# SP issues the vectors' transfers, ScalarE's operands run one chunk ahead of its squares, and the first unit's remainder and the vectors' transposes stand later

## The chip, the core and the metric

The kernel runs on one core of a Trainium2 chip. The core has TensorE (PE), VectorE (DVE), ScalarE (ACT), GpSimd (POOL) and SyncE (SP), which run their own instruction streams and meet at semaphores. The metric is the device time of one execution in microseconds; the figure is the median of the runs.

## What is computed

A float32 layer of 512 tokens by 1024 features (sparse attention beside a gated convolution, cross attention and a gated feed-forward), followed by a second block of two layers (a state space mixer, a forgetting attention, two feed-forwards). The change touches the first norm and the first projection:

```python
def rmsnorm(x, g):
    xf = x.astype(jnp.float32)
    y = xf * lax.rsqrt(jnp.mean(xf * xf, axis=-1, keepdims=True) + EPS)
    return (y * g.astype(jnp.float32)).astype(x.dtype)

h = rmsnorm(x, norm_mix_g)
proj = h @ w_in
q, k, v, qi, ki, wi, glu = jnp.split(proj, cuts, axis=-1)
q = partial_rope(q.reshape(bsz, seq, A_HEADS, HEAD_DIM), cos, sin)
```

## The kernel before

Every engine's order is written out by hand, and every dependence is a semaphore. The activations lie with features on partitions: X has eight chunks (`KC`) of 128 features by 512 tokens. A projection is a row of units. A unit makes 128 output features: SP loads its weights into RAW (two slots), ScalarE rounds them into WH (`round_weights`, semaphore `w_hi`), GpSimd makes the rest WL = RAW - WH (`remainder`, `w_lo`), and TensorE sums WH by the rounded operand PH and WH by its rest PL over the eight chunks, sixteen matmuls, then WL by PH, eight more (`unit`). These are called the high matmuls and the remainder phase below. Up to unit 7 a unit is one column block of `w_in`. SP may load the weights of unit u only when WL of unit u - 2 is made.

In the head of the program the vectors (gains, biases, convolution taps: fifteen small inputs in `VECTORS`) are loaded as rows into VROW, and turned by TensorE into columns. `norm_mix_g` comes first, alone (`gain_in`), so that `vec_c` 1 lets the operands start; the others are turned by three transposes, VectorE copies them to VEC, and that is `vec_c` 2. x comes in four transfers into XROW. TensorE turns each chunk (`turn_x`), VectorE copies it to X (`x_ready`), ScalarE makes PH = X * gain rounded (`op_hi`) and the square SQ of the chunk, VectorE makes PL (`low`, `op_lo`), and GpSimd adds the square to SSQ (`add_square`, `sq_used`). SQ has two slots, so the square of chunk c waits for the sum of chunk c - 2. In `prepare` this wait stands ahead of PH too.

The norm's scale does not enter the operands. It is applied when a unit's result leaves PSUM: `column_sums` sums SSQ over partitions on TensorE, VectorE and ScalarE make the inverse root and a diagonal DIAG, `spread_scales` spreads it over partitions inside unit 1, between the high matmuls and the remainder phase, and VectorE copies it to RS. Then VectorE takes units 0 and 1 out of PSUM and goes on to the angles of the rotation (`angles`).

Behind the squares ScalarE rounds two constants, waits for `vec_c` 2, issues four small transfers that swap halves of the taps and biases (WSW, BSW), and then rounds the weights of unit 1.

Of the kernel before, what the change touches and what calls it, by code (L numbers as in the profile page):

```python
# [20 lines left out]
ACT = mybir.ActivationFunctionType  # L21
AX = mybir.AxisListType.X

P = 128
T = 512
TB = T // P
D = 1024
KC = D // P
# [49 lines left out]
ROWS = [0, 0, 0]  # L78
COLUMN = {}
# [47 lines left out]
def build_program(nc, A, out):  # L127
    ctx = ExitStack()
    with ctx:
# [12 lines left out]
        X = at("X", [P, KC, T], F32, 0)  # L142
        PH = at("PH", [P, KC, T], F32R, 16384)
        PL = at("PL", [P, KC, T], F32R, 32768)
# [48 lines left out]
        VROW = at("VROW", [P, 3, P], F32, 155648)  # L193
        POSI = at("POSI", [P, T], I32, 163840)
# [114 lines left out]
        IDENT, ROTM, TRI, ONES = (CST[:, i * P:(i + 1) * P] for i in range(4))  # L309
# [5 lines left out]
        def column(name, i):  # L315
            name, first = name if isinstance(name, tuple) else (name, 0)
            t, base = COLUMN[name][0], COLUMN[name][1] + first
            return VEC[:, t, bass.ds(base + i, 1)]
# [166 lines left out]
        def _(sp):  # L485
# [9 lines left out]
            for j, c in enumerate(IN_COLS):  # L495
                load(START["in"] + j, j % 2, w_in[:, :, c:c + P])
                if j == 1:
                    sp.dma_start(MROW[:], A["mem"][0].rearrange("(b p) d -> p b d", p=P)).then_inc(mem_in, 16)
            with sp.Fori(0, 4) as i:
                for s in range(2):  # L500
# [122 lines left out]
        def _(act):  # L623
# [6 lines left out]
            def prepare(norm, c, gain, hi, s, ready):  # L630

                square_free(norm, c)
                act.wait_ge(*ready)
                act.activation(hi, X[:, bass.ds(c, 1), :], ACT.Copy, scale=column(gain, c)).then_inc(op_hi, 1)
                act.activation(SQ[:, s, :], X[:, bass.ds(c, 1), :], ACT.Square).then_inc(sq_ready, 1)  # L635
# [10 lines left out]
                act.wait_ge(st_var, NORM[norm] + 1)  # L646
                act.activation(SDN, VN, ACT.Sqrt).then_inc(st_std, 1)

            for name, rows, t in VECTORS:
                r = COLUMN[name][1]  # L650
                flat = A[name] if len(A[name].shape) == 1 else A[name].rearrange(
                    "a b -> (a b)") if len(A[name].shape) == 2 else A[name].rearrange("a b c -> (a b c)")
                act.dma_start(VROW[r:r + rows, t, :], flat.rearrange("(r p) -> r p", p=P))\
                   .then_inc(gain_in if name == "norm_mix_g" else vec_in, 16)
            act.dma_start(POSI[:], A["positions"].to_broadcast([P, T])).then_inc(pos_in, 16)
            act.wait_ge(vec_c, 1)
            for c in range(KC):
                prepare("mix", c, "norm_mix_g", PH[:, c, :], c % 2, (x_ready, c + 1))
                if c == 3:
                    round_weights(0, 0)  # L660
            act.wait_ge(cst_in, 16)
# [586 lines left out]
        def _(pool):  # L1248
            def remainder(u, s, kc=KC):
                pool.wait_ge(w_hi, u + 1)  # L1250
                pool.tensor_tensor(WL[:, s, 0:kc], RAW[:, s, 0:kc], WH[:, s, 0:kc], ALU.subtract).then_inc(w_lo, 1)  # L1251
# [5 lines left out]
            def add_square(norm, c, s):  # L1257
                pool.wait_ge(sq_ready, SQUARES[norm] + c + 1)
                if isinstance(c, int) and c == 0:
                    if NORM[norm]:  # L1260
                        pool.wait_ge(st_sum, NORM[norm])
                    pool.tensor_copy(SSQ[:], SQ[:, s, :]).then_inc(sq_used, 1)
                else:
                    pool.tensor_tensor(SSQ[:], SSQ[:], SQ[:, s, :], ALU.add).then_inc(sq_used, 1)  # L1264
                pool.drain()  # L1265
# [4 lines left out]
            pool.memset(VSH[0][:].bitcast(F32), 0.0).then_inc(pad_zero, 1)  # L1270
            pool.memset(VSL[0][:].bitcast(F32), 0.0).then_inc(pad_zero, 1)
            for c in range(KC):
                add_square("mix", c, c % 2)
                if c == 3:
                    remainder(0, 0)
            for u in range(1, 4):
                remainder(u, u % 2)
            pool.wait_ge(wc_hi, 1)
# [330 lines left out]
        def _(pe):  # L1609
# [25 lines left out]
            def column_sums(norm):  # L1635

                pe.wait_ge(sq_used, SQUARES[norm] + dict(NORMS)[norm])
                if NORM[norm]:
                    pe.wait_ge(st_rs, NORM[norm])
                for b in range(TB):  # L1640
                    mm = pe.matmul(ST[:, b:b + 1], SSQ[:, b * P:(b + 1) * P], ONES[:, 0:1], start=True, stop=True)
                mm.then_inc(st_sum, 1)

            def spread_scales(norm):

                pe.wait_ge(st_diag, NORM[norm] + 1)
                pe.matmul(ST[:], ONES, DIAG[:], start=True, stop=True).then_inc(st_bc, 1)
# [12 lines left out]
            pe.transpose(ST[:, 0:KC], VROW[0:KC, 0, :], IDENT[0:KC, 0:KC]).then_inc(vec_t, 1)  # L1660
            for c in range(KC):
                turn_x(c)
            pe.wait_ge(vec_in, 16 * (len(VECTORS) - 1))
            pe.wait_ge(vec_c, 1)
            for t in range(3):
                mm = pe.transpose(ST[:, t * P:t * P + ROWS[t]], VROW[0:ROWS[t], t, :], IDENT[0:ROWS[t], 0:ROWS[t]])
            mm.then_inc(vec_t, 1)

            def rotate(j):
                rows = P if j not in (0, 3) else 64  # L1670
# [37 lines left out]
                    mm.then_inc(mem_t, 1)  # L1708

            unit(0, 0, PH, PL, chunks=(op_lo, NOPERAND["mix"]))  # L1710
            pe.wait_ge(vec_c, 2)
            column_sums("mix")
            unit(1, 1, PH, PL, between=lambda: spread_scales("mix"))
            unit(2, 0, PH, PL)
            turn_weights_in()
            rotate(0)
# [1432 lines left out]
```

## Time and profile before

| | us |
|---|---|
| median of 3 runs | 2082.72 |
| lowest and highest | 2082.22, 2085.34 |
| profiled execution, whole | 2086.91 |
| its span, first to last instruction | 2085.1 |

The rows of the trace are times in microseconds from the start of the span: when a group of instructions starts, how long it takes, its engine, its line in the kernel, the operation, and in brackets how long the engine had been idle before it and what ended that. An engine name with a q (ACTq, SPq) is the queue that issues a transfer. TensorE's durations are modelled and overlap; the distance between two starts is the time that one takes of the engine. Matmuls are named by the buffers: PH,WH and PL,WH are the high matmuls, PH,WL the remainder phase.

### The profile page before, as it was taken

To read this page: it belongs to the slowest core of one execution; us is meant where nothing else is said; L and a number is where in the kernel's file an instruction comes from. 1 tells how busy PE (TensorE), PEld (TensorE's weight loads), DVE (VectorE), ACT (ScalarE), POOL (GpSimd) and SP (SyncE) were. 2 spreads that over 40 slices of the span, in tenths; PEclk is the share of its full clock that TensorE was granted. 3 is DMA by queue.
4 is the path that set the end of the run, shared out by engine and by line. 5 is a ranking of instruction groups with operands and counts; after the bars stand their busy time and mean duration, and the time that the engine had idled before them with its cause. 6 is when DMAs were issued, how large, how long until landed. Compare 5 with 4: busy or idle time off the path is not lost.

```text
span 2085.1 us, 31481 instructions
## 1 busy us (share of the span) xinstructions
PE 1975.9 (95%) x10763; PEld 1628.5 (78%) x10763; DVE 1053.7 (51%) x1640; ACT 742.7 (36%) x1263; POOL 1058.9 (51%) x591
## 2 busy tenths in 40 slices
PE   8989888999999999789999999999999899999997
PEld 5678866778877888567778888887878788888886
DVE  6797743745687686798342213132126723122132
ACT  4335444443322223445432222233237732222223
POOL 5575626536756644690554444446445264444442
PEclk9999999999999999999999999999999999999999
DMA  4334103142333332100323333334346333333332
GB/s 136 80 109 110 26 25 89 54 81 85 97 101 90 96 96 80 51 2 13 101 81 101 93 99 95 96 93 107 92 116 144 91 99 94 91 100 93 99 96 85
DMA packets 345028, 181.87 MB, mean 87 GB/s; under 512 B 28527, under 2 KB 336103, under 8 KB 344935
## 3 DMA queue, kind: packets, MB, share of 16 engines
q1 hardware_dynamic: 343872, 179.91, 31.4%
q8 instruction: 55, 0.90, 0.2%
q10 hardware_dynamic: 1062, 0.75, 0.1%
q14 instruction: 39, 0.31, 0.0%
HBM read 162.73 MB, written 2.10 MB: 79 GB/s over the span
## 4 chain that ended last, share of the span: by engine, by line
PE 56%; issue 12%; DVE 9%; POOL 8%; POOLq 5%; ACT 3%; DVEq 3%; DMA 1%; SPq 1%; ACTq 0%
PE ACC L1621 16%; PE ACC L1627 15%; PE ACC L1622 15%; POOL WL L1251 7%; POOLq L1265 2%; DVE SC L2410 1%; POOLq L1475 1%; POOLq L1463 1%; PE ACC L1793 1%; PE ST L2093 1%; DVE M L2407 1%; POOL GC L1474 1%; PE O L1750 1%; PE ST L1750 1%; PE O L1752 1%
## 5 line engine op out<-in xcount | busy, mean ns | idle before, releaser
L1251 POOL TENSOR_TENSOR WL<-RAW,WH 128x1024 fp32r<-128x1024 f32 (+1 forms) x292 | 691.6, 2371 | 738.3 <-ACT WH L628 680.8
L1621 PE MATMUL ACC<-PH,WH 128*128 128x512 f32 x1248 | 494.4, 396 | 7.0 <-DVE PL L2203 1.6
L1622 PE MATMUL ACC<-PL,WH 128*128 128x512 f32 x1248 | 488.6, 391 | 0.0
L628 ACT ACTIVATE WH<-RAW 128x1024 fp32r<-128x1024 f32 (+1 forms) x292 | 300.8, 1032 | 452.9 <-PE ACC L1627 402.4
L1621 PE MATMUL ACC<-QH,WH 128*128 128x512 f32 (+1 forms) x1136 | 430.2, 383 | 19.9 <-ACT WH L628 10.4
L1622 PE MATMUL ACC<-QL,WH 128*128 128x512 f32 (+1 forms) x1136 | 425.4, 379 | 0.0
L1627 PE MATMUL ACC<-PH,WL 128*128 128x512 f32 x1248 | 312.7, 393 | 0.0
L1621 PEld LDWEIGHTS ACC<-PH,WH 128*128 128x128 f32 x1248 | 235.8, 189 | 65.1 <-issue 4.8
L1627 PE MATMUL ACC<-QH,WL 128*128 128x512 f32 (+1 forms) x1136 | 271.7, 380 | 9.6 <-POOL WL L1251 6.4
L1627 PEld LDWEIGHTS ACC<-PH,WL 128*128 128x128 f32 x1248 | 235.1, 189 | 52.8 <-issue 3.3
L1622 PEld LDWEIGHTS ACC<-PL,WH 128*128 128x128 f32 x1248 | 235.8, 189 | 48.7 <-issue 1.0
L1621 PEld LDWEIGHTS ACC<-QH,WH 128*128 128x128 f32 x1136 | 214.7, 189 | 70.0 <-issue 14.5
L1627 PEld LDWEIGHTS ACC<-QH,WL 128*128 128x128 f32 x1136 | 205.7, 189 | 53.9 <-POOL WL L1251 10.9
L1622 PEld LDWEIGHTS ACC<-QL,WH 128*128 128x128 f32 x1136 | 214.9, 189 | 38.4 <-issue 0.2
L3020 DVE TENSOR_TENSOR X<-X,ACC 128x512 f32 x48 | 33.0, 687 | 216.3 <-PE ACC L1627 216.3
L3010 DVE TENSOR_TENSOR H<-ACC,RS 128x512 f32<-128x512 f32 x64 | 44.3, 692 | 149.1 <-PE ACC L1627 148.6
L1264 POOL TENSOR_TENSOR SSQ<-SSQ,SQ 128x512 f32<-128x512 f32 x51 | 74.3, 1458 | 69.2 <-ACT SQ L635 64.3
L876 ACT ACTIVATE QH<-H 128x512 f32 (+1 forms) x54 | 34.1, 632 | 158.2 <-DVE H L3012 128.3
L2496 DVE TENSOR_TENSOR PTL<-ACC,PTH 128x128 fp32r<-128x128 f32 (+2 forms) x112 | 53.4, 476 | 37.3 <-ACT PTH L816 36.9
L816 ACT ACTIVATE PTH<-ACC 128x128 fp32r<-128x128 f32 (+2 forms) x112 | 47.8, 427 | 60.6 <-PE O L1752 36.8
L876 ACT ACTIVATE PH<-H 128x512 f32 (+1 forms) x32 | 20.2, 632 | 128.3 <-DVE H L3012 128.3
L2832 DVE TENSOR_TENSOR QL<-H,QH 128x512 f32 x54 | 37.4, 693 | 49.4 <-ACT QH L876 49.4
(450 smaller groups left out, 2566.4 us busy)
## 6 DMA issues: line engine op xcount, KB each, us to landing
RAW<-in_mlp_w_dram SPq DMA_DIRECT2D x128, 512.0 KB, 4.0
RAW<-in_w_gate_dram SPq DMA_DIRECT2D x22, 512.0 KB, 3.7
RAW<-in_w_up_dram SPq DMA_DIRECT2D x22, 512.0 KB, 3.8
RAW<-in_w_in_dram SPq DMA_DIRECT2D x16, 512.0 KB, 3.9
RAW<-in_w_down_dram SPq DMA_DIRECT2D x16, 512.0 KB, 4.0
RAW<-in_ssm_w_glu_dram SPq DMA_DIRECT2D x16, 512.0 KB, 3.8
RAW<-in_w_kvf_dram SPq DMA_DIRECT2D x16, 512.0 KB, 3.9
RAW<-in_w_out_dram SPq DMA_DIRECT2D x16, 256.0 KB, 2.8
```

The source lines that it names most:

```text
L628: act.activation(WH[:, s, 0:kc], RAW[:, s, 0:kc], ACT.Copy).then_inc(w_hi, 1)
L816: act.activation(parts(kind, t // TB)[0][:, first:first + kb, qb * P:(qb + 1) * P], TT[t % 2][:, 0:kb * P].rearrange("p (k q) -> p k q", q ...
L876: act.activation(hi[:, bass.ds(k, 1), :], to, ACT.Copy).then_inc(hid_hi, 1)
L1251: pool.tensor_tensor(WL[:, s, 0:kc], RAW[:, s, 0:kc], WH[:, s, 0:kc], ALU.subtract).then_inc(w_lo, 1)
L1264: pool.tensor_tensor(SSQ[:], SSQ[:], SQ[:, s, :], ALU.add).then_inc(sq_used, 1)
L1265: pool.drain()
L1621: pe.matmul(ACC[s][:, 0:n], WH[:, s, k, :], xh[:, k, :], start=(k == 0), stop=False)
L1622: pe.matmul(ACC[s][:, 0:n], WH[:, s, k, :], xl[:, k, :], start=False, stop=False)
L1627: mm = pe.matmul(ACC[s][:, 0:n], WL[:, s, k, :], xh[:, k, :], start=False, stop=(k == kc - 1))
L1750: pe.matmul(out, ah, bh, start=first, stop=False)
L2496: dve.tensor_tensor(pair[1][to], TT[t % 2][:, 0:kb * P].rearrange("p (k q) -> p k q", q=P), pair[0][to], ALU.subtract).then_inc(pt_lo, 1)
L3010: dve.tensor_tensor(h[:], ACC[s][:], RS[:], ALU.mult).then_inc(unit_out, 1)
```

## The change

Four things move; no arithmetic is added or removed.

- The transfers of fourteen vectors and of the positions go from ScalarE's queue to SP's, behind the weights of units 0 and 1 and ahead of `mem`. `norm_mix_g` stays on ScalarE's queue.
- ScalarE makes PH of chunk c + 1 ahead of the square of chunk c, and only the square waits for its slot.
- GpSimd makes the remainder of unit 0 after six sums of squares instead of four.
- TensorE turns the vectors behind unit 0 instead of ahead of it, and the column sums go from between units 0 and 1 into unit 1, ahead of its fifth chunk.

```diff
@@ SP
                 if j == 1:
+                    for name, rows, t in VECTORS:
+                        r = COLUMN[name][1]
...
+                        if name != "norm_mix_g":
+                            sp.dma_start(VROW[r:r + rows, t, :], flat.rearrange("(r p) -> r p", p=P)).then_inc(vec_in, 16)
+                    sp.dma_start(POSI[:], A["positions"].to_broadcast([P, T])).then_inc(pos_in, 16)
                     sp.dma_start(MROW[:], A["mem"][0].rearrange("(b p) d -> p b d", p=P)).then_inc(mem_in, 16)
@@ ScalarE
-            for name, rows, t in VECTORS:
...
-            act.dma_start(POSI[:], A["positions"].to_broadcast([P, T])).then_inc(pos_in, 16)
+            act.dma_start(VROW[0:KC, 0, :], A["norm_mix_g"].rearrange("a b -> (a b)").rearrange("(r p) -> r p", p=P)).then_inc(gain_in, 16)
             act.wait_ge(vec_c, 1)
-            for c in range(KC):
-                prepare("mix", c, "norm_mix_g", PH[:, c, :], c % 2, (x_ready, c + 1))
+            for c in range(KC + 1):
+                if c < KC:
+                    act.wait_ge(x_ready, c + 1)
+                    act.activation(PH[:, c, :], X[:, c, :], ACT.Copy, scale=column("norm_mix_g", c)).then_inc(op_hi, 1)
+                if c:
+                    square("mix", c - 1, X, (c - 1) % 2)
                 if c == 3:
                     round_weights(0, 0)
@@ GpSimd
             for c in range(KC):
+                if c == 6:
+                    remainder(0, 0)
                 add_square("mix", c, c % 2)
-                if c == 3:
-                    remainder(0, 0)
@@ TensorE
-            pe.wait_ge(vec_in, 16 * (len(VECTORS) - 1))
-            pe.wait_ge(vec_c, 1)
-            for t in range(3):
-                mm = pe.transpose(ST[:, t * P:t * P + ROWS[t]], VROW[0:ROWS[t], t, :], IDENT[0:ROWS[t], 0:ROWS[t]])
-            mm.then_inc(vec_t, 1)
+            def turn_vectors():
...
+            def first_sums():
+                pe.wait_ge(vec_c, 2)
+                column_sums("mix")
             unit(0, 0, PH, PL, chunks=(op_lo, NOPERAND["mix"]))
-            pe.wait_ge(vec_c, 2)
-            column_sums("mix")
-            unit(1, 1, PH, PL, between=lambda: spread_scales("mix"))
+            turn_vectors()
+            unit(1, 1, PH, PL, inside=(4, first_sums), between=lambda: spread_scales("mix"))
```

On TensorE, at the end of unit 0 and the start of unit 1 (ST<-CST,SSQ are the column sums), before:

```order
L1627 MATMUL ACC<-PH,WL 128x512 x8
L1641 MATMUL ST<-CST,SSQ 128x1 x4
L1621 MATMUL ACC<-PH,WH 128x512
L1622 MATMUL ACC<-PL,WH 128x512
L1621 MATMUL ACC<-PH,WH 128x512
```

And now, from the remainder phase of unit 0 to the fifth chunk of unit 1 (ST<-CST,VROW are the vectors' transposes):

```order
L1632 MATMUL ACC<-PH,WL 128x512 [waits w_lo]
L1632 MATMUL ACC<-PH,WL 128x512 x7
L1672 MATMUL ST<-CST,VROW 128x100 [waits vec_c,vec_in]
L1672 MATMUL ST<-CST,VROW 128x124
L1672 MATMUL ST<-CST,VROW 128x88
L1626 MATMUL ACC<-PH,WH 128x512 [waits w_hi]
...
L1627 MATMUL ACC<-PL,WH 128x512
L1646 MATMUL ST<-CST,SSQ 128x1 [waits sq_used,vec_c]
L1646 MATMUL ST<-CST,SSQ 128x1 x3
```

The transposes stand between the two units now, and four chunks of unit 1 stand ahead of the sums.

On ScalarE, the middle of the chunks, before:

```order
L634 ACTIVATE PH<-X,VEC 128x512 [waits x_ready,sq_used]
L635 ACTIVATE SQ<-X 128x512
L628 ACTIVATE WH<-RAW 128x1024 [waits w_landed0]
L634 ACTIVATE PH<-X,VEC 128x512 [waits x_ready,sq_used]
L635 ACTIVATE SQ<-X 128x512
```

And now, from there to the weights of unit 1:

```order
L661 ACTIVATE PH<-X,VEC 128x512 [waits x_ready]
L650 ACTIVATE SQ<-X 128x512 [waits sq_used]
L635 ACTIVATE WH<-RAW 128x1024 [waits w_landed0]
...
L650 ACTIVATE SQ<-X 128x512 [waits sq_used] x2
L667 ACTIVATE PAIR<-CST 128x128 [waits cst_in]
L668 ACTIVATE PAIR<-CST 128x128
L672 DMA WSW<-VEC 64x124 [waits vec_c]
L673 DMA BSW<-VEC 64x4
L672 DMA WSW<-VEC 64x124
L673 DMA BSW<-VEC 64x4
L635 ACTIVATE WH<-RAW 128x1024 [waits w_landed1]
```

The wait for the slot went from PH to SQ. The rows from PAIR to WH are the same as before; the `vec_c` that they wait for comes from the transposes above.

## Rows read from the trace of the kernel before

**Rows 1.** The page: the chain that ended last, by engine.

```profile
PE 56%; issue 12%; DVE 9%; POOL 8%; POOLq 5%; ACT 3%; DVEq 3%; DMA 1%; SPq 1%; ACTq 0%
```

**Rows 2.** The chain in order of time, 25 to 60: start, us, what.

```profile
25.67 3.33 PE ACC L1627 x8
...
34.43 1.87 PE ACC L1627 x8
...
37.99 0.43 DVE COS L2287
...
38.50 2.67 DVE COS L2289
...
58.22 0.70 PE FOUR L1696 x4
```

**Rows 3.** Timeline of TensorE, 13 to 37.

```profile
17.08 0.73 PE L1666 MATMUL ST<-CST,VROW 100*128 100x100 f32 x3
17.53 0.78 PE L1621 MATMUL ACC<-PH,WH 128*128 128x512 f32 x1
...
21.94 0.40 PE L1621 MATMUL ACC<-PH,WH 128*128 128x512 f32 x1
...
24.86 0.50 PE L1621 MATMUL ACC<-PH,WH 128*128 128x512 f32 x1 [0.97 <-DVE PL L2203]
...
28.84 0.95 PE L1641 MATMUL ST<-CST,SSQ 128*128 128x1 f32 x8
29.65 0.47 PE L1621 MATMUL ACC<-PH,WH 128*128 128x512 f32 x1
```

**Rows 4.** Busy time by window; behind POOL's stands the granted clock (PEclk).

```profile
26.00:27.00 1.00, 1.00 (x4) 0.81 (x3) 0.00 (x0) 0.00 (x0) 0.00 (x0) 0.50 0.13 32
```

**Rows 5.** Timeline of ScalarE and its queue, 7 to 30.

```profile
7.58 0.43 ACTq L655 DMA_DIRECT2D POSI<-in_positions_dram  x1
8.09 1.28 ACT L634 ACT_TABLE_LOAD   x1 [8.09 <-DVE X L2249]
...
14.58 1.06 ACT L628 ACTIVATE WH<-RAW 128x1024 fp32r<-128x1024 f32 x1
...
16.15 0.61 ACT L635 ACTIVATE SQ<-X 128x512 f32<-128x512 f32 x1
...
21.15 0.72 ACT L634 ACTIVATE PH<-X,VEC 128x512 fp32r<-128x512 f32 x1 [3.23 <-POOL SSQ L1264]
...
25.35 0.53 ACTq L667 DMA_DIRECT2D WSW<-VEC  x1
...
27.86 1.06 ACT L628 ACTIVATE WH<-RAW 128x1024 fp32r<-128x1024 f32 x1 [3.62 <-issue]
```

**Rows 6.** Timeline of VectorE, 6 to 37.

```profile
6.57 0.69 DVE L2249 COPY X<-FOUR 128x512 f32<-128x512 f32 x1 [2.39 <-PE FOUR L1655]
...
15.44 0.68 DVE L2249 COPY X<-FOUR 128x512 f32<-128x512 f32 x1
...
24.73 0.59 DVE L2256 COPY VEC<-ST 128x92 f32<-128x92 f32 x3
...
31.42 0.69 DVE L2235 TENSOR_TENSOR DIAG<-CST,ST 128x512 f32<-128x512 f32 x1
```

**Rows 7.** Timeline of GpSimd, 6 to 39.

```profile
15.12 1.52 POOL L1264 TENSOR_TENSOR SSQ<-SSQ,SQ 128x512 f32<-128x512 f32 x1 [0.16 <-issue]
16.81 2.62 POOL L1251 TENSOR_TENSOR WL<-RAW,WH 128x1024 fp32r<-128x1024 f32 x1 [0.16 <-issue]
...
38.49 2.40 POOL L1251 TENSOR_TENSOR WL<-RAW,WH 128x1024 fp32r<-128x1024 f32 x1 [4.66 <-ACT WH L628]
```

**Rows 8.** Timeline of SP's queue, 0 to 40.

```profile
3.34 4.30 SPq L489 DMA_DIRECT2D RAW<-in_w_in_dram  x2
```

**Rows 9.** DMA of 0 to 30: GB/s in 40 slices, and RAW: KB, median us to landing.

```profile
GB/s 0 0 100 272 308 336 241 317 341 359 376 378 333 306 290 295 305 314 338 375 386 311 158 66 16 0 0 80 255 322 42 0 0 0 0 42 1 43 1 0
...
RAW<-in_w_in_dram SPq DMA_DIRECT2D x3, 512.0 KB, 11.2
```

More of the change, by code:

```diff
@@ L497, in _ @@
                 if j == 1:
+                    for name, rows, t in VECTORS:
+                        r = COLUMN[name][1]
+                        flat = A[name] if len(A[name].shape) == 1 else A[name].rearrange(
+                            "a b -> (a b)") if len(A[name].shape) == 2 else A[name].rearrange("a b c -> (a b c)")
+                        if name != "norm_mix_g":
+                            sp.dma_start(VROW[r:r + rows, t, :], flat.rearrange("(r p) -> r p", p=P)).then_inc(vec_in, 16)
+                    sp.dma_start(POSI[:], A["positions"].to_broadcast([P, T])).then_inc(pos_in, 16)
                     sp.dma_start(MROW[:], A["mem"][0].rearrange("(b p) d -> p b d", p=P)).then_inc(mem_in, 16)
@@ L647, in standard_deviation @@
                 act.activation(SDN, VN, ACT.Sqrt).then_inc(st_std, 1)
-            for name, rows, t in VECTORS:
[L650 to L654, printed above, removed]
-            act.dma_start(POSI[:], A["positions"].to_broadcast([P, T])).then_inc(pos_in, 16)
-            act.wait_ge(vec_c, 1)
-            for c in range(KC):
-                prepare("mix", c, "norm_mix_g", PH[:, c, :], c % 2, (x_ready, c + 1))
+            act.dma_start(VROW[0:KC, 0, :], A["norm_mix_g"].rearrange("a b -> (a b)").rearrange("(r p) -> r p", p=P)).then_inc(gain_in, 16)
+            act.wait_ge(vec_c, 1)
+            for c in range(KC + 1):
[4 more added lines that the diff above has]
+                    square("mix", c - 1, X, (c - 1) % 2)
                 if c == 3:
@@ L1662, in _ @@
                 turn_x(c)
-            pe.wait_ge(vec_in, 16 * (len(VECTORS) - 1))
-            pe.wait_ge(vec_c, 1)
-            for t in range(3):
-                mm = pe.transpose(ST[:, t * P:t * P + ROWS[t]], VROW[0:ROWS[t], t, :], IDENT[0:ROWS[t], 0:ROWS[t]])
-            mm.then_inc(vec_t, 1)
+            def turn_vectors():
+                pe.wait_ge(vec_in, 16 * (len(VECTORS) - 1))
+                pe.wait_ge(vec_c, 1)
+                for t in range(3):
+                    mm = pe.transpose(ST[:, t * P:t * P + ROWS[t]], VROW[0:ROWS[t], t, :], IDENT[0:ROWS[t], 0:ROWS[t]])
+                mm.then_inc(vec_t, 1)
+            def first_sums():
+                pe.wait_ge(vec_c, 2)
+                column_sums("mix")
             def rotate(j):
```

## The prediction

> **What bounds the kernel now.** The page comes first: the chain that ended last lies to 56% on TensorE [rows 1]. The change touches only the head of the program, so the head's part of that chain is read next [rows 2]. It passes through the remainder phase of unit 0 (25.67), through unit 1 up to the end of its remainder phase (34.43 + 1.87 = 36.30), then through VectorE, which takes unit 1 out and makes the angles (37.99, 38.50), and it is back on TensorE at 58.22. So one number decides: the time at which unit 1 ends, 36.30 now. What follows hangs on it by waits of one engine on another, with nothing tied to an absolute time; I pass a shift on one to one.
>
> How 36.30 comes about is read backwards in the timelines. Unit 1's first matmul is at 29.65, right behind the column sums of 28.84, which stand behind unit 0's remainder phase [rows 3]. That phase took 3.33 us where the same eight matmuls of unit 1 take 1.87 [rows 2], because the granted clock was 0.50, the 1.2 GHz level [rows 4]. TensorE had waited before it for VectorE's PL (the last wait 0.97 us, [rows 3]), because ScalarE's seventh PH had waited 3.23 us for GpSimd's SSQ [rows 5]: GpSimd was in the 2.62 us remainder of 16.81 [rows 7].
>
> **1. Vectors leave ScalarE's queue.** ScalarE issues DMAs until 8.01 and loads its table at 8.09 [rows 5]. X of chunk 0 is ready at 6.57 + 0.69 = 7.26 [rows 6]. With one DMA to issue it starts at 7.3: 0.8 us earlier, PH of chunk 0 at 8.6. The fourteen vectors and POSI now stand on SP's queue behind the second RAW load, whose issue ends at 3.34 + 4.30 = 7.64 [rows 8]. At 0.43 us each, as for POSI [rows 5], their issue lasts to 14.1 and the transfer of `mem`, behind them, is issued 6.4 us later. With the 11.2 us that the crowded loads took [rows 9] it lands at 25, against a use on ScalarE beyond 31, and the vectors are wanted at 25.4 (below). Both are hidden, at no cost.
>
> The 0.42 MB of vectors and POSI no longer run beside x and RAW of unit 0. RAW 0 was issued at 3.34 and landed 11.2 later, at 14.54 [rows 8, 9], and ScalarE's rounding of it begins at 14.58 [rows 5]: it waited for the transfer. At 300 GB/s, about the mean of the slices up to 14 us (241 to 378), 0.42 MB (304 rows of 512 bytes and 128 copies of 2 KB) are 1.4 us, so the landing lies between 13.2 and 14.5; I take the middle, 13.9. The Trainium skill, page "DMA: Bandwidth & Descriptors", section "Issuing engines are not separate DMA queues", says that DMAs of different issuers run on the same 16 engines and interleave, so that moving an issue saves only the sequencer's time. By it the landing is 13.2; were the queues apart, it stays 14.5, and every time of the next step moves by 0.7 with it.
>
> **2. PH ahead of the square, remainder later.** ScalarE reaches the rounding of unit 0 at 13.2 and stands there until 13.9. From the start of that rounding to the end of the next square it takes 16.15 + 0.61 - 14.58 = 2.18 us [rows 5], so the square of chunk 3 ends at 16.1. GpSimd then adds squares 3, 4 and 5 back to back, 1.69 us apart (15.12 to 16.81, [rows 7]), and the remainder starts at 21.2. With the 2.40 of a remainder in the clear (38.49) it ends at 23.6. TensorE: X of chunk 5 was copied at 15.44 [rows 6] and goes with the head by 0.8, so unit 0 starts at about 16.6 in place of 17.53. There are eleven matmuls between 17.53 and 21.94, 0.43 apart, and at the full clock they stand 1.87 / 8 = 0.23 apart. Of sixteen, ten at 0.43 and six at 0.23 or 0.43 end between 22.3 and 23.5. PL is ready: VectorE takes 1.7 us a chunk, so from X of chunk 5 at 14.6 the last PL is done near 21. The remainder phase therefore waits for GpSimd until 23.6 and takes 1.87 at the full clock: unit 0 ends at **25.4**, where it ended at 29.0. That is the gain, 3.6 us.
>
> **3. The vectors' transposes behind unit 0.** Here it is given back. ScalarE's order is not changed behind the squares: it waits for `vec_c` 2, issues four DMAs, and only then rounds the weights of unit 1. Before, VEC was copied at 24.73, the first of the DMAs began at 25.35 and the rounding at 27.86 [rows 5, 6], all beside unit 0's slow remainder phase. Now the transposes (0.73 us, 17.08 in [rows 3]) follow unit 0, the copies (0.59) follow them, then 27.86 - 25.35 = 2.51 of issues and 1.06 of rounding: 25.4 + 0.73 + 0.59 + 2.51 + 1.06 + 0.15 for four handovers = **30.4**. Unit 1 starts 0.75 us later than before. TensorE is idle from 26.1 to 30.4, and queued behind unit 1 on it is all the rest.
>
> **4. The sums inside unit 1.** Before, the chain from the sums (ended 28.84 + 0.95 = 29.79) to DIAG (31.42 + 0.69 = 32.11, [rows 6]) ran under unit 1's sixteen high matmuls, 3.8 us, free of charge. Now it has only the last eight, 1.86 us, as cover, and it takes 2.32. The spread takes 0.9, what is left of the 36.30 - 29.65 = 6.65 us of unit 1 without its 3.8 and 1.87. Unit 1: 1.86 + 0.7 for the sums (the 0.95 lies partly at the low clock) + 2.3 + 0.9 + 1.87 = 7.65 us in place of 6.65. That is +1.0. The sums' own 0.7 is no new work, it stood ahead of the unit before.
>
> **5. The clock.** TensorE's idle 4.3 us ahead of unit 1 have no like in the head. The nearest row is the drop to 0.50 after a stretch in which it was only partly idle [rows 3, 4], so I expect unit 1 to start at 1.2 GHz. Such a spell lasted 3.0 us (about 25.5 to 28.5) and, at the start, 4.4 us (17.53 to 21.94); half of it is lost, 1.5 to 2.2. Part of it falls into the wait for DIAG: I take **+1.7**; the ends are 0 and 2.5. The Trainium skill, "TensorE: Matmul & The Clock Gate", Part 1, says "the default state is throttled, and activity releases the throttle". By it the 1.7 stands; with the clock held it would be 0 and the sum 1.75.
>
> **Sum.** 0.75 + 1.0 + 1.7 = +3.45 us: unit 1 ends at 39.75 instead of 36.30. The profiled execution took 2086.9 around its span of 2085.1 and would become 2090.4; it lies 4.2 above the median of the runs, 2082.7, and the median would become **2086.2**.
>
> **Rivals.**
> *The clock holds.* The idle stretch is too short, or the engine recovers in the first matmuls. For it: the drop before came only after several gaps, of which the last was 0.97. Against it: 4.3 us in one piece. +1.75 us, 2084.5.
> *Slow through unit 1* (the other side). If the low level outlasts the first half, the sums and all twenty-four matmuls run at 0.43 instead of 0.23: 24 x 0.2 = 4.8 in place of 1.7, and the sum is 0.75 + 1.0 + 4.8 = +6.55, 2089.3. It decides from a spell of over 7 us on. GpSimd's remainder of unit 3 works the same way from another side: one VectorE step of the angles lies under it and takes 2.67 us where the like step ahead of it takes 0.43 (38.50, 37.99 in [rows 2]; the remainder is 38.49 in [rows 7]). Another alignment catches two such steps, +2.2, or none, -2.2.
> *The gain stays.* If the four DMA issues take the 0.43 us of POSI's each, 1.7 in place of 2.51, unit 1 starts at 29.6, and with the clock held and no collision with the angles the sum is 3.45 - 0.8 - 1.7 - 2.2 = -1.25, 2081.5. A gain beyond 4 us needs more still.
> *It doesn't do what it says.* If the vectors land after 25.4, behind two RAW loads, TensorE waits for them: 1 us of lateness costs 1 us. RAW 1 is issued by 7.64 and, 11.2 later, through by 18.8 at the latest, and they are small; some 6 us are in hand.
>
> **How the numbers follow.** Forecast 0.50 (+1.7 to +4.8), clock holds 0.20, slow through unit 1 or two collisions 0.20, gain stays 0.07, late vectors 0.03. A measurement of this kernel tells about 0.2%, 4.2 us, from no change. Of the forecast 0.08 lie beyond it; with 0.20 and 0.02 that is slower 0.30. Faster by 4.2 us has no mechanism here beyond the unknown alignments: 0.05. The rest, 0.65, is within. Low end: the gain-stays case, -1.25; high end: the slow spell, +6.55. With 0.4 of scatter below, 2081.0, and the rest of it left out above, 2089.2.
>
> **What would show it.** In the profile of the changed kernel: table load at about 7.3; rounding of unit 0 at 13.2 to 14.5; no wait of PH on SSQ; the remainder of unit 0 ending near 23.6; a TensorE gap of some 4 us ahead of unit 1, its matmuls 0.43 apart at first; a wait for DIAG in unit 1; its end near 39.75. Wrong would be: the rounding of unit 1 ahead of the transposes, or a shift at 36 us that is not found at 58 us and at the end.

## The result and the profile after

The kernel after takes 2092.07 us (median of 5 runs, 2091.69 to 2093.04), the kernel before 2082.72 in the same rounds (5 runs, 2081.86 to 2087.06): ratio 1.0040, with an interval of 1.0027 to 1.0052. It is slower by more than the 0.2% that the prediction counted as no change, and 5.9 us above the predicted 2086.2, beyond the range's 2089.2. Later rounds put it at 1.0027 (1.0017 to 1.0036). Between medians the loss is 9.4 us in the first rounds and 5.9 in the later ones; 5.9 above 2082.7 would lie just inside the range. The profiled execution took 2091.69 around a span of 2089.9.

The mechanism that the prediction named is there. The timeline of TensorE from unit 0 to unit 2, after (the lines left out are matmuls of the same units; compare [rows 3]):

```profile
17.14 0.78 PE L1626 MATMUL ACC<-PH,WH 128*128 128x512 f32 x1
...
24.43 0.50 PE L1626 MATMUL ACC<-PH,WH 128*128 128x512 f32 x1 [2.04 <-DVE PL L2212]
...
25.00 2.00 PE L1632 MATMUL ACC<-PH,WL 128*128 128x512 f32 x8
26.84 0.44 PE L1672 MATMUL ST<-CST,VROW 100*128 100x100 f32 x3
31.56 0.80 PE L1626 MATMUL ACC<-PH,WH 128*128 128x512 f32 x1 [4.29 <-ACT WH L635]
32.16 0.63 PE L1627 MATMUL ACC<-PL,WH 128*128 128x512 f32 x1
32.59 0.63 PE L1626 MATMUL ACC<-PH,WH 128*128 128x512 f32 x1
...
35.15 1.70 PE L1646 MATMUL ST<-CST,SSQ 128*128 128x1 f32 x8
...
40.27 1.43 PE L1652 MATMUL ST<-DIAG,CST 128*128 128x512 f32 x2
41.13 2.39 PE L1632 MATMUL ACC<-PH,WL 128*128 128x512 f32 x8
43.50 0.47 PE L1626 MATMUL ACC<-PH,WH 128*128 128x512 f32 x1
```

Unit 0 ends at 26.84 (before: 28.84, both read at the start of what follows its remainder phase). Then TensorE waits 4.29 us for the rounded weights of unit 1, and unit 1 runs from 31.56 to 43.50: 11.94 us, where it was 6.6 (29.65 in [rows 3] to 36.3). Its high matmuls stand 0.43 apart. The granted clock, by window (the columns are us, busy time of PE, PEld, DVE, ACT and POOL, then PEclk, DMA share and GB/s):

```profile
30.00:31.00 1.00, 0.00 (x0) 0.00 (x0) 0.00 (x0) 0.55 (x1) 0.00 (x0) 0.92 0.13 32
31.00:36.00 5.00, 4.44 (x13) 3.67 (x14) 0.00 (x0) 1.79 (x2) 2.37 (x1) 0.50 0.16 32
36.00:40.00 4.00, 4.00 (x12) 3.32 (x13) 1.55 (x6) 2.83 (x5) 1.71 (x1) 0.50 0.31 92
...
41.00:42.00 1.00, 1.00 (x4) 0.57 (x3) 0.27 (x1) 0.00 (x0) 0.00 (x0) 0.96 0.20 26
```

A window of 1 us with a mean between the two levels tells where the edge lies: 0.92 is a fall 0.16 us before its end, at 30.84, and 0.96 a rise 0.08 us behind its start, at 41.08. So the clock falls to 1.2 GHz in the idle stretch and is back at 2.4 GHz 10.2 us later, 9.5 us into the unit: it stays low through all sixteen high matmuls, the sums and the spread, although TensorE is busy from 31.56 on without a break.

Why unit 1 started at 31.56 stands on ScalarE and its queue, after (compare [rows 5]):

```profile
7.46 1.28 ACT L661 ACT_TABLE_LOAD   x1 [7.46 <-DVE X L2258]
...
13.61 1.04 ACT L635 ACTIVATE WH<-RAW 128x1024 fp32r<-128x1024 f32 x1
...
27.95 0.53 ACTq L672 DMA_DIRECT2D WSW<-VEC  x1
...
29.79 0.62 ACTq L673 DMA_DIRECT2D BSW<-VEC  x1
30.45 1.06 ACT L635 ACTIVATE WH<-RAW 128x1024 fp32r<-128x1024 f32 x1 [8.15 <-issue]
```

ScalarE's operands no longer wait for GpSimd (the 3.23 us of [rows 5] are gone), and the engine has nothing to do for 8.15 us but wait for `vec_c` 2 and issue four transfers, with the weights of unit 1 unrounded behind them. On VectorE, the last three PL, the vectors' copies and DIAG, after:

```profile
18.33 1.17 DVE L2212 SCALAR_TENSOR_TENSOR PL<-X,VEC,PH 128x512 fp32r<-128x512 f32 x1
...
20.03 4.35 DVE L2212 SCALAR_TENSOR_TENSOR PL<-X,VEC,PH 128x512 fp32r<-128x512 f32 x2
27.31 0.60 DVE L2265 COPY VEC<-ST 128x92 f32<-128x92 f32 x3 [2.94 <-PE ST L1672]
...
38.28 0.69 DVE L2244 TENSOR_TENSOR DIAG<-CST,ST 128x512 f32<-128x512 f32 x1
```

The view of the tile PL, of 21.3 to 21.6, splits the pair of 20.03 (minimum, median and maximum in ns, first and last start): the last PL began at 21.5 and took 2.85 us, until 20.03 + 4.35 = 24.38.

```profile
L2212 DVE SCALAR_TENSOR_TENSOR PL<-X,VEC,PH x2: 1577/2212/2848, 20.0 to 21.5; 128x512 fp32r<-128x512 f32 x2
```

And on GpSimd, the remainder of unit 0, after (compare [rows 7]):

```profile
21.21 2.61 POOL L1256 TENSOR_TENSOR WL<-RAW,WH 128x1024 fp32r<-128x1024 f32 x1 [0.16 <-issue]
```

The shift at the end of unit 1, 43.5 - 36.3 = +7.2, is found again where [rows 2] ended. In the chain of waits, after, the line that stood at 58.22 is 7.0 us later:

```profile
65.24 0.70 PE FOUR L1706 x4
```

The first transposes of `mem` also come 7.0 us later (97.16 before, 104.16 after). Beyond them the two executions do not keep this distance: at the sums of the next norm it is 2.7 us, and at the end 4.8. Those sums, before and then after:

```profile
357.28 0.95 PE L1641 MATMUL ST<-CST,SSQ 128*128 128x1 f32 x8
```

```profile
359.94 0.95 PE L1646 MATMUL ST<-CST,SSQ 128*128 128x1 f32 x8
```

The change does not touch this stretch. From the first transposes of `mem` to these sums the profiled executions of all kernels here take between 254.3 and 260.1 us (before 260.1 and 259.4, after 255.8 and 256.2), so a difference of the order of the effect comes from there. The mean granted clock of 200 to 300 us was 0.90 in the execution of before and 0.93 in that of after. A single pair of spans therefore doesn't measure the change. The medians do (+9.4 and +5.9), and up to 97 us the heads do.

### The profile page after: what moved, and what is told of

It is laid out like the page before. It is cut to its first block, busy times and chain, and to the rows that moved or that the text cites. A ratio compares the mean times of both kernels' runs of the same rounds, so it can differ in the third digit from the quotient of the medians.

```text
span 2089.9 us, 31475 instructions
## 1 busy us (share of the span) xinstructions
PE 1977.1 (95%) x10763; PEld 1628.8 (78%) x10763; DVE 1051.8 (50%) x1640; ACT 743.0 (36%) x1263; POOL 1058.8 (51%) x591
## 4 chain that ended last, share of the span: by engine, by line
PE 55%; issue 13%; POOL 10%; DVE 7%; POOLq 6%; ACT 3%; DVEq 2%; DMA 2%; SPq 1%; ACTq 0%
PE ACC L1626 16%; PE ACC L1627 15%; PE ACC L1632 15%; POOL WL L1256 7%; POOLq L1270 2%; POOLq L1480 1%; POOLq L1468 1%; PE ACC L1802 1%; PE ST L2102 1%; POOL GC L1479 1%; PE ST L1759 1%; PE O L1759 1%; ACT WH L635 1%; PE O L1761 1%; POOL GT L1467 1%
## 5 line engine op out<-in xcount | busy, mean ns | idle before, releaser
L1626 PE MATMUL ACC<-PH,WH 128*128 128x512 f32 x1248 | 497.1, 398 | 11.5 <-ACT WH L635 4.5
L881 ACT ACTIVATE PH<-H 128x512 f32 (+1 forms) x32 | 20.2, 632 | 128.3 <-DVE H L3021 128.3
```

What stands on the lines that cost most here:

```text
L881: act.activation(hi[:, bass.ds(k, 1), :], to, ACT.Copy).then_inc(hid_hi, 1)
L1626: pe.matmul(ACC[s][:, 0:n], WH[:, s, k, :], xh[:, k, :], start=(k == 0), stop=False)
```

## The experiments

Names: the "head" of a run is the start of unit 2's first matmul in its profile, when unit 1 is done (before 36.2, after 43.5). The theory: TensorE's late transposes make the whole loss, through the wait for `vec_c` 2 that holds up the rounding of unit 1, and the low clock behind that wait. Rivals: the loss comes from the other parts (SP's queue, ScalarE's or GpSimd's order), or from the sums inside unit 1. Each ratio is to the kernel before in the same rounds, where its median was 2083.87 to 2084.04.

**before_again**: the kernel before, unchanged, as a control.

> The kernel before, unchanged, for a second execution with a profile. The profile shown of before took 2086.9 us, 4.2 above the median of its runs. If the head alone makes the difference between the two kernels, unit 1 ends at 36.3 us here too, and what executions of before differ in lies further on, in the spells of the low clock between 180 and 295 us, of which a quick execution should show fewer. If instead the head of the shown execution was unusual, unit 1 ends elsewhere than at 36.3 by more than 1 us.

Measured: 2084.02 (2080.88 to 2086.80), ratio 1.0004 (0.9995 to 1.0013). Its executions scatter by 6 us. In this one unit 0's remainder phase ran at the full clock, and the head is at 34.95, not 36.2:

```profile
24.81 1.98 PE L1627 MATMUL ACC<-PH,WL 128*128 128x512 f32 x8
26.63 0.95 PE L1641 MATMUL ST<-CST,SSQ 128*128 128x1 f32 x8
28.36 0.50 PE L1621 MATMUL ACC<-PH,WH 128*128 128x512 f32 x1 [0.78 <-ACT WH L628]
```

So the slow remainder phase of [rows 2], from which the prediction read the gain of step 2, is met in some executions only. In the shown execution of before its row is:

```profile
25.47 3.54 PE L1627 MATMUL ACC<-PH,WL 128*128 128x512 f32 x8
```

It was worth less than it seemed: here unit 1 waits for ScalarE even with the fast phase.

**round1_first**: the weights of unit 1 rounded ahead of the wait for `vec_c` 2.

```diff
+            round_weights(1, 1)
             act.wait_ge(vec_c, 2)
...
-            rounded(1)
```

> The changed kernel with one line moved: ScalarE rounds the weights of unit 1 behind the two constants and ahead of the wait for the vectors' columns and the four small transfers. Theory that these issues, behind the late transposes, hold unit 1: the rounding runs at about 22.3 to 23.4, unit 1 starts right behind the transposes at 27.6, in place of 31.56, the clock stays up, unit 1 takes 7.7 us in place of 11.9 and ends near 35.3 to 36, so the time falls by 7 to 8 us against the changed kernel, to about 2084, near before. Rival, that the two units are held apart by the transposes and sums on TensorE itself: less than 2 us gained.

Measured: 2085.30 (2078.79 to 2089.37), ratio 1.0005 (0.9995 to 1.0016); head 36.16. TensorE, with nothing idle ahead of unit 1 and now a wait inside it:

```profile
26.39 0.44 PE L1672 MATMUL ST<-CST,VROW 100*128 100x100 f32 x3
26.62 0.48 PE L1626 MATMUL ACC<-PH,WH 128*128 128x512 f32 x1
...
33.23 1.12 PE L1652 MATMUL ST<-DIAG,CST 128*128 128x512 f32 x2 [1.79 <-DVE DIAG L2244]
```

One line moved on ScalarE takes 7.3 us from the head and brings the time back to that of before. So most of what the late transposes cost in the head goes through the rounding behind the issues. Not all of it: the four issues (27.51 to about 29.97) stand now ahead of the square root of the norm, whose table load begins at 30.00, and DIAG is late for it. With TensorE's old order and the same rounding (early_round1 below) the head is 1.9 us earlier and the median 4.9 lower. Only the 1.9 is seen in the head; the profiled execution of round1_first took 2081.08, 4.2 below its median, and where the rest of the 4.9 lies isn't shown.

**gap_filled**: the kernel after with eighteen superfluous matmuls behind the transposes, in what was idle time. Their result is overwritten.

```diff
             turn_vectors()
+            for _ in range(18):
+                pe.matmul(ACC[1][:], WH[:, 0, 0, :], PH[:, 0, :], start=True, stop=True)
```

> The changed kernel with 18 extra matmuls (first weights of unit 0 by the first chunk, into the bank that unit 1 starts over) between the transposes and unit 1; the wait for the weights of unit 1 stays. 18 x 0.23 = 4.1 us fill the gap of 4.3 us, so that unit 1 still starts at 31.6 to 31.8. Theory that the low clock through unit 1 costs 4 us more than the wait itself: the clock stays at 2.4 GHz, unit 1 takes 7.7 us and ends at 39.3, the time falls by 4 us to about 2088. Rival, that the idle stretch alone is the price and the clock is only seen beside it: no gain, or a loss.

Measured: 2087.22 (2085.91 to 2089.44), ratio 1.0018 (1.0009 to 1.0027). The matmuls fill the wait and unit 1 follows at once, at the full clock:

```profile
28.09 4.55 PE L1723 MATMUL ACC<-PH,WH 128*128 128x512 f32 x18
32.67 0.50 PE L1626 MATMUL ACC<-PH,WH 128*128 128x512 f32 x1
...
40.69 0.47 PE L1626 MATMUL ACC<-PH,WH 128*128 128x512 f32 x1
```

```profile
32.00:36.00 4.00, 3.96 (x22) 3.08 (x21) 0.17 (x1) 2.08 (x4) 2.39 (x1) 1.00 0.03 4
```

Unit 1 takes 8.0 us instead of 11.9, so the clock costs it 3.9 us. Unit 1 starts 1.1 us later than in after, 0.8 of it because unit 0 ended later (27.65; its remainder phase was slow in this execution, 3.23 us), and the head is 2.8 earlier. With the wait filled, the clock holds through unit 1. In the three executions with 4.29 us of idle time ahead of unit 1 (after, after_again, turns_late_only) and in sums_outside, with 2.54, unit 1 began at the low clock; in the others, with 0.78 at most, at the full one. So unit 1's clock goes with the idle time ahead of it here, though a fall also came with less: at 25.1 in this run, at 25.4 in before, behind waits of 2.04 and 0.97 us, and in turns_late_only at 24.2, ahead of the 4.29. In medians the gain is smaller and less sure than in the head: 2.5 us against the later rounds of after, with intervals that overlap (1.0009 to 1.0027 and 1.0017 to 1.0036), and 4.9 against the first.

**turns_early**: the kernel after with TensorE's order as it was before (transposes ahead of unit 0, sums between the units).

```diff
+            pe.wait_ge(vec_in, 16 * (len(VECTORS) - 1))
+            pe.wait_ge(vec_c, 1)
...
             unit(0, 0, PH, PL, chunks=(op_lo, NOPERAND["mix"]))
-            turn_vectors()
-            unit(1, 1, PH, PL, inside=(4, first_sums), between=lambda: spread_scales("mix"))
+            first_sums()
+            unit(1, 1, PH, PL, between=lambda: spread_scales("mix"))
```

> The changed kernel with TensorE's order as before: the vectors' transposes ahead of unit 0, the column sums between units 0 and 1. The vectors still come over SP's queue. Theory that the late transposes hold the weights of unit 1: rounding of unit 1 ends before unit 0 does, and unit 1 starts right behind the sums at about 28 to 29; against that the transposes wait for vectors that SP issued last at 15.5, to land at 17.5 to 18.5, so unit 0 starts 1 us later. Unit 1 ends near 36, 7 us earlier than changed, time 2084 to 2086. Rival, that the gain is lost to SP's queue: the transposes wait until after 20 and unit 1 ends beyond 38.

Measured: 2080.58 (2078.80 to 2082.57), ratio 0.9988 (0.9979 to 0.9996): faster than before, 9.2 and 11.5 us below the two medians of after, and 3.4 below the low end of what was expected. Its head:

```profile
23.80 0.50 PE L1626 MATMUL ACC<-PH,WH 128*128 128x512 f32 x1 [1.61 <-DVE PL L2211]
...
24.37 2.00 PE L1632 MATMUL ACC<-PH,WL 128*128 128x512 f32 x8
27.91 0.50 PE L1626 MATMUL ACC<-PH,WH 128*128 128x512 f32 x1 [0.40 <-ACT WH L635]
...
34.49 0.47 PE L1626 MATMUL ACC<-PH,WH 128*128 128x512 f32 x1
```

The three other parts are a small gain, and TensorE's part undoes it. Unit 1 is again released by ScalarE's WH, as in before_again. The head explains only a part of the 3.4 us between the medians: it is 1.7 us earlier than in the shown execution of before and 0.5 earlier than in before_again.

**turns_late_only**: the kernel before with TensorE's part of the change alone.

```diff
             unit(0, 0, PH, PL, chunks=(op_lo, NOPERAND["mix"]))
-            pe.wait_ge(vec_c, 2)
-            column_sums("mix")
-            unit(1, 1, PH, PL, between=lambda: spread_scales("mix"))
+            turn_vectors()
+            unit(1, 1, PH, PL, inside=(4, first_sums), between=lambda: spread_scales("mix"))
```

> The kernel before with TensorE's part of the change alone: transposes behind unit 0, sums inside unit 1; vectors on ScalarE's queue, the squares and the remainder as before. Theory that TensorE's part makes the whole loss: the weights of unit 1 come behind unit 0, transposes, copies and four issues, unit 1 starts 4.7 us after unit 0 at 31.5 to 33.7, runs at the low clock and ends at 43.5 to 45.5; time 2092 to 2094, as changed or a little above. Rival, that the loss needs the vectors on SP's queue or the late remainder: below 2088.

Measured: 2091.77 (2090.05 to 2093.70, 6 runs), ratio 1.0036 (1.0023 to 1.0048), as slow as the whole change. The wait for WH is again 4.29 us, with everything but TensorE's order as in before:

```profile
34.43 0.80 PE L1621 MATMUL ACC<-PH,WH 128*128 128x512 f32 x1 [4.29 <-ACT WH L628]
...
37.96 0.95 PE L1641 MATMUL ST<-CST,SSQ 128*128 128x1 f32 x8
...
44.01 0.47 PE L1621 MATMUL ACC<-PH,WH 128*128 128x512 f32 x1
```

With turns_early this settles where the loss comes from, from both sides. The low clock ended here 3.4 us into unit 1, ahead of the sums (0.95 us for them, where after has 1.70), but it had been low since 24.2, through unit 0's remainder phase (3.62 us), 13.6 us in all.

**sums_outside**: the kernel after with the sums ahead of unit 1, in the idle time.

```diff
             turn_vectors()
-            unit(1, 1, PH, PL, inside=(4, first_sums), between=lambda: spread_scales("mix"))
+            first_sums()
+            unit(1, 1, PH, PL, between=lambda: spread_scales("mix"))
```

> The changed kernel with the column sums ahead of unit 1 (behind the transposes) instead of inside it; everything else, the gap ahead of unit 1 too, stays. In the changed kernel unit 1 starts at 31.6 and the clock is back up only at about 40.7; the sums stand in the middle, 1.6 us of one-column matmuls. Theory that the sums inside the unit prolong the slow spell: with sixteen matmuls in one piece the clock is up after 3 to 5 us, the second half runs at 0.23 apart, unit 1 ends at 39.5 to 40.5, 3 to 4 us earlier than changed, time near 2088.5. Rival, that the spell after such a gap lasts 9 us whatever follows: only the 1.6 us of the sums leave unit 1, it ends near 42, time near 2090.5.

Measured: 2088.35 (2082.91 to 2091.04), ratio 1.0019 (1.0009 to 1.0028); head 40.70.

```profile
31.40 0.79 PE L1626 MATMUL ACC<-PH,WH 128*128 128x512 f32 x1 [2.54 <-ACT WH L635]
...
40.70 0.47 PE L1626 MATMUL ACC<-PH,WH 128*128 128x512 f32 x1
```

Unit 1 starts when it did, still slow, but takes 9.3 us in place of 11.9. 1.6 of the 2.6 are the sums, which lie in idle time now; the rest is the clock, low from 30.4 to 37.3, 6.8 us instead of 10.2:

```profile
37.00:38.00 1.00, 1.00 (x5) 0.78 (x5) 0.00 (x0) 0.00 (x0) 0.00 (x0) 0.87 0.56 104
```

In these heads the place of the sums is a second, smaller part of the loss. The medians do not show it: 2088.35 lies 1.4 us below the later median of after, and the intervals overlap. The head was a little later than the 39.5 to 40.5 expected.

**after_again**: the kernel after, unchanged, as a control.

> The changed kernel once more, for a second execution with a profile and for its time beside before in the same rounds. In its first profile the slow spell of unit 1 lasted from before 31 to 40.7, across the sums; with the sums ahead of the unit it ended at 37.1, with them inside but a remainder phase that was slow already it ended at 37.6. If the long spell belongs to the sums' place, unit 1 ends at 43 to 44 again. If the end of a spell falls by chance, unit 1 ends anywhere between 39.5 and 44, and the times of the rounds scatter by 3 us or more. In the rounds of the first result they lay within 1.4 us of each other, which speaks for the former. Expected: 2091 to 2093.

Measured: 2089.76 (2086.32 to 2093.99, 12 runs), ratio 1.0027 (1.0017 to 1.0036). The head is at 42.57. Unit 1 starts at 31.12 and the clock is low from 29.4 to 39.6, again 10.2 us, but 1.7 of them lie in the idle stretch where the first execution had 0.7:

```profile
29.00:30.00 1.00, 0.00 (x0) 0.00 (x0) 0.00 (x0) 0.00 (x0) 0.00 (x0) 0.69 0.05 3
39.00:40.00 1.00, 1.00 (x4) 0.79 (x3) 0.00 (x0) 1.00 (x2) 1.00 (x1) 0.69 0.00 0
```

The spell has the same length in both executions of this code, and what differs is when it begins. The time is below the 2091 to 2093 expected, and the executions scatter by 8 us, where the expectation named a scatter of 3 us or more as the sign that a spell's end falls by chance; the head, 42.57, lies between its two cases. Two equal lengths don't rule the chance out.

**early_round1**: turns_early and round1_first together. Beside the edit of turns_early:

```diff
+            round_weights(1, 1)
             act.wait_ge(vec_c, 2)
...
-            rounded(1)
```

> The kernel with SP's vectors, ScalarE's order and the late remainder, TensorE's order as before, and the rounding of unit 1's weights ahead of the wait for the vectors' columns. Without it (turns_early) TensorE waited 0.4 us for that rounding at 27.9. Theory: unit 1 starts at 27.5, right behind the sums, the rest of it is bound by matmuls; 0.4 us gained, time about 2080.2. Rival, that ScalarE's four issues now stand between the rounding and the square root (the table load waits behind them) and DIAG comes late: no gain or 1 us lost.

Measured: 2080.39 (2079.13 to 2084.66), ratio 0.9984 (0.9975 to 0.9993); head 34.23, unit 1 starts at 27.68.

**early_remainder4**: turns_early with the remainder of unit 0 after four sums of squares, as before, to let VectorE's last PL go free.

```diff
-                if c == 6:
+                if c == 4:
                     remainder(0, 0)
```

> turns_early with the remainder of unit 0 after four sums of squares, as before, instead of six. In turns_early the last PL of VectorE stands behind that remainder and TensorE waits 1.6 us for it at 23.8. Theory that the late remainder only moves the collision of VectorE and GpSimd from one PL to another: the remainder at 17.2 holds up PL of chunk 5 and the X behind it instead, the last PL comes at the same time within 0.5 us, time 2080 to 2081.5. If the late remainder was a gain by itself, it is 1 us or more slower; if it was a loss, 1 us or more faster.

Measured: 2080.28 (2079.18 to 2084.45), ratio 0.9987 (0.9978 to 0.9996); head 34.61. TensorE's wait for the last PL falls from 1.61 to 0.95 us, but the PL that now lies under the remainder is an earlier one, and the remainder phase starts at 24.45, as in turns_early:

```profile
18.18 2.26 DVE L2211 SCALAR_TENSOR_TENSOR PL<-X,VEC,PH 128x512 fp32r<-128x512 f32 x1
```

**early_both**: turns_early with the edits of both.

```diff
+            round_weights(1, 1)
             act.wait_ge(vec_c, 2)
...
-            rounded(1)
@@ GpSimd
-                if c == 6:
+                if c == 4:
                     remainder(0, 0)
```

> early_round1 and early_remainder4 together: SP's vectors, ScalarE's order, remainder of unit 0 after four sums, rounding of unit 1 ahead of the wait for the vectors' columns, TensorE's order as before. If what each of the two brings is real and separate, the last PL comes at 23.9, unit 1 starts at 27.4 and ends near 34; time 2079.5 to 2080.5. If nothing is left to gain in this stretch, it equals turns_early within 0.5 us.

Measured: 2080.41 (2077.41 to 2084.27), ratio 0.9991 (0.9982 to 1.0001); head 33.92. The three versions and turns_early have heads 0.7 us apart at most and medians within 0.3 us; they can't be told apart by their times. The gain over before is in what they share.

**vectors_sp_only**: the kernel before with the vectors' and positions' transfers on SP, as in the change, and nothing else.

```diff
@@ SP
                 if j == 1:
+                    for name, rows, t in VECTORS:
...
+                    sp.dma_start(POSI[:], A["positions"].to_broadcast([P, T])).then_inc(pos_in, 16)
@@ ScalarE
-            for name, rows, t in VECTORS:
...
-            act.dma_start(POSI[:], A["positions"].to_broadcast([P, T])).then_inc(pos_in, 16)
```

> The kernel before with the vectors and positions issued by SP alone; ScalarE's order, the remainder and TensorE's order as before. Theory that turns_early's gain of 3.4 us comes from both parts: here ScalarE's table load starts at 7.4 in place of 8.1, the rounding of unit 0 at 13.5 in place of 14.6, but PH of chunk 6 still waits for GpSimd's sums behind the remainder. Unit 0 starts 0.3 to 0.7 us earlier, unit 1 ends at 34.5 to 36; time 2082 to 2084. Rival, that this part makes the whole gain: 2080 to 2081.

Measured: 2082.11 (2079.59 to 2085.35), ratio 0.9992 (0.9983 to 1.0001); head 35.56, both as expected. Its table load still begins at 8.09: here x came late (the copy of chunk 0 began at 7.31 and ended at 8.00, where it ended at 7.26 in before), and not the queue held ScalarE. PH waits for GpSimd as before:

```profile
21.16 0.72 ACT L641 ACTIVATE PH<-X,VEC 128x512 fp32r<-128x512 f32 x1 [3.24 <-POOL SSQ L1265]
```

**order_only**: the kernel before with ScalarE's and GpSimd's orders of the change.

```diff
@@ ScalarE
-            for c in range(KC):
-                prepare("mix", c, "norm_mix_g", PH[:, c, :], c % 2, (x_ready, c + 1))
+            for c in range(KC + 1):
...
+                if c:
+                    square("mix", c - 1, X, (c - 1) % 2)
@@ GpSimd
+                if c == 6:
+                    remainder(0, 0)
                 add_square("mix", c, c % 2)
-                if c == 3:
-                    remainder(0, 0)
```

> The kernel before with ScalarE's order (PH ahead of the last chunk's square) and the late remainder alone; vectors on ScalarE's queue, TensorE's order as before. Theory as above: ScalarE starts at 8.1, PH no longer waits for sums, the last PL still collides with the remainder. Unit 1 ends at 34.5 to 36; time 2081 to 2083. Rival, that the order makes the whole gain of turns_early: 2080 to 2081.

Measured: 2082.64 (2078.52 to 2086.51), ratio 0.9995 (0.9984 to 1.0007); head 34.79, both as expected. The collision that was expected did not come: in this run the last PL was nearly done when the late remainder began (21.88), and TensorE waited for the remainder itself:

```profile
24.54 2.11 PE L1631 MATMUL ACC<-PH,WL 128*128 128x512 f32 x8 [1.48 <-POOL WL L1255]
```

The two parts alone are 1.8 and 1.2 us below before's median of 2083.9 and neither is clear of no change; together (turns_early) they make 3.4 (2083.95 to 2080.58). Beside before_again's head of 34.95 those of the two, 35.56 and 34.79, show no gain.

## Why the prediction was wrong

The sum was 0.75 + 1.0 + 1.7 = +3.45 at the end of unit 1. The measured shift is +7.2. It passed on one to one, as assumed, at 58 and at 97 us. At the end of the two shown executions it is +4.8, so the shift at 36 us is not found whole at the end, which the prediction had named as a sign of being wrong. What stands behind that is the scatter between 97 us and the end, which the sum did not have. By its steps:

**Step 1 was right in its results, and one reading in it was wrong.** The table load began at 7.46 (7.3 said), the rounding of unit 0 at 13.61 (13.9 said), and vectors and `mem` were hidden: no unit waited for a vector, though SP's issues of vectors and positions lasted to 15.85 and not to 14.1. But the rounding of before did not wait for the transfer, as the step said. Its row has no idle time, and it begins where the square ahead of it ends (13.95 + 0.61 = 14.56):

```profile
13.95 0.61 ACT L635 ACTIVATE SQ<-X 128x512 f32<-128x512 f32 x1
```

In after too it stands right behind a square, with no idle time. That 13.61 is near 13.9 is luck. In before_again the rounding did wait for RAW (0.74 us, until 14.71).

**Step 2 was right about GpSimd and wrong about VectorE.** The remainder ran from 21.21 to 23.82, against 21.2 to 23.6. But the step said "the last PL is done near 21": it was done at 24.38. A part of this is that X did not come earlier: chunk 5 was copied at 15.64 (14.6 said, 15.44 before) and unit 0 started at 17.14 (16.6 said). The last PL began at 21.5, just behind the remainder's start, and took 2.85 us. The two ahead of it, which lay beside sums of GpSimd, took 1.58 and 1.17, and the first, at 9.51 with nothing on GpSimd, 0.75. The rows that would have told it were at hand: the rival *slow through unit 1* priced such a collision (2.67 us against 0.43, [rows 2]) for another place, and I did not look for it here. The Trainium skill, page "SBUF — State Buffer", section "🔬 SBUF: two separate sides", says that the port pair that VectorE and GpSimd share is an exclusive lock for a whole instruction, and that a VectorE operation with two SBUF inputs needs it against a GpSimd operation that reads SBUF. The trace agrees within 0.2 us: this PL ends 0.56 us behind the 2.61 us remainder, where waiting for its whole length would leave the 0.75 of a PL alone. Unit 0's end came 1.45 us later than the 25.4 forecast (26.84). Of the expected 3.6 us, 2.0 were gained on the shown execution of before, and nothing on before_again, whose unit 0 ends at 26.63.

**Step 3 was right, and it is the cause.** Transposes, copies, issues and rounding put unit 1 at 4.72 us behind unit 0's end (5.0 said); turns_late_only and turns_early show that TensorE's order alone makes the loss, and round1_first that it acts in the main through the rounding behind the issues. With unit 0 late by 1.45, unit 1 starts 31.56 - 29.65 = 1.9 us later than before, not 0.75.

**Step 4: the +1.0 did not come as a wait.** At half clock the last eight high matmuls took 3.6 us, long enough for DIAG (ready at 38.97, spread at 40.27). The sums took 1.56 instead of 0.7. The test of this step is gap_filled, with the same order at the full clock: the wait for DIAG is there, 0.22 us, and unit 1 takes 8.0 where 7.65 was said. (The 1.79 us of round1_first are longer because the issues stand ahead of the square root there.) My division of unit 1 into 3.8, 0.9 and 1.87 was also off: read from starts, the spread takes 0.46 and the remainder phase 2.4, in both kernels.

**Step 5 is the step that failed: the term for the clock was mis-sized.** +1.7 was taken from spells of 3.0 and 4.4 us. The spell took 10.2 us, 9.5 of them in the unit. Its price, from the starts: high matmuls 7.15 us against 3.76 (+3.4), sums 1.56 against 0.81 (+0.75), spread 0.86 against 0.46 (+0.4), together 4.5. gap_filled, without the spell, gives 3.9 of it back. With start +1.9, sums 0.8 moved into the unit and 4.5 of clock the shift of 7.2 is complete. Against the +3.45 that was said, 2.8 us of the miss are this term, and 1.15 are unit 0's late end from step 2.

The 4.4 us were also misread. They run from the first matmul of unit 0, not from the start of a spell. In before and in all but two of the runs the granted clock reads 1.00 there, though the matmuls stand 0.43 apart. Two runs have the spell in their rows, 6.8 us long, and it begins some 4 us ahead of unit 0: from 13.0 to 19.9 in early_round1, from 13.4 to 20.2 in vectors_sp_only. early_round1:

```profile
13.00:14.00 1.00, 0.00 (x0) 0.00 (x0) 1.00 (x2) 1.00 (x2) 0.71 (x2) 0.51 0.14 34
14.00:19.00 5.00, 4.04 (x15) 3.38 (x16) 5.00 (x6) 3.69 (x7) 3.39 (x3) 0.50 0.53 116
19.00:20.00 1.00, 1.00 (x5) 0.77 (x3) 1.00 (x3) 0.56 (x2) 0.56 (x1) 0.57 0.95 371
```

The four transposes of a chunk of x took 0.66 us at 12.16 in that run, ahead of the fall, and 1.09 at 14.46, behind it. In before the chunk at 14.58 took 1.08: TensorE was slow well ahead of 17.53 there too. So the spell at the start was longer than it was read.

The rival *slow through unit 1* named the condition that was met (a spell of over 7 us); it had 0.20. Its 4.8 is near the 4.5 by luck: it counts the eight matmuls of the remainder phase, which ran at the full clock (2.37 us), and leaves out what the sums and the spread lost.

**From the head to the median.** The prediction laid its shift on an execution whose head (36.2) was itself slowed; before_again had 34.95. The two heads of after are 43.50 and 42.57, so the change costs between 6.3 and 8.6 us in the head, and 5.9 and 9.4 in the medians. This is a part that I could have bounded: an execution 4.2 above the median has its loss somewhere, and the low clock of [rows 4] was one place.

**What stays open**: what sets the length of the low spell. Read from its edges it was 3.4 us in before (25.4 to 28.8) and in gap_filled (25.1 to 28.5), 6.8 at the start of early_round1 and vectors_sp_only, 6.8 with the sums ahead of unit 1, 10.2 and 10.2 with the sums inside, and 13.6 in turns_late_only, where it began in unit 0. The length of the wait (4.29 against 0.69 and 2.54) changed together with the place of the sums, and no run parted the two. Also open is what part of the 3.4 us gain is due to each of the two remaining parts, and where the 1.7 to 2.9 us of it arise that the head does not show.

## What to carry to other kernels

When work is moved behind something on one engine, follow its result to the next engine and list all that is queued behind the wait there, transfer issues included: here four issues of 0.6 us and a rounding stood between a moved transpose and the next unit of matmuls. Price an idle stretch of some 4 us on TensorE by the work that follows at half clock (3.4, 8.5 and 9.5 us of it here), and not by the shortest spell in the trace. And when a GpSimd operation is moved, look which VectorE operation it now lies beside.

## What was not expected of the hardware

- The clock stayed low for 9.5 and 8.5 us of unbroken matmuls behind a 4.29 us wait, and was low from the first of them; in turns_early, with no wait over 1.61 us, the granted clock was 1.00 from 24 to 34 us.
- The last PL took 2.85 us (0.75 with nothing on GpSimd) beside the 2.61 us remainder, which began ahead of it, and an earlier remainder only moved the delay to an earlier PL (2.26 us in early_remainder4).
- Executions of one kernel scatter by 6 to 11 us (before_again 2080.88 to 2086.80, after_again 2086.32 to 2093.99, round1_first 2078.79 to 2089.37). Unit 0's remainder phase took 1.98 or, at the low clock, 3.54 us in two executions of the kernel before.
- At the start of before, and of most runs, the matmuls stand 0.43 us apart while the granted clock reads 1.00; in early_round1 and vectors_sp_only it reads 0.50 over matmuls that stand so. A granted clock of 1.00 in a row did not exclude slow matmuls there.
